# Moving the weight slots and the matmul inputs of a 16-bit-split float32 transformer kernel within SBUF

## The chip, the cores and the metric

The kernel runs on one core of one Trainium2 chip. The metric is the device time of one execution in microseconds (us). A time is the median of several executions; the profile is of one more execution, whose own time is given beside its span.

## The reference, cut to what matters

The input is one sequence of 512 tokens with 1024 features. A first block of four mixers, then two hybrid layers (attention, RWKV-7, retention), each with a feed-forward part. Nearly all arithmetic is in products of the activations with large weight matrices:

```
def first_block(...):
    h = rms_norm(x, norm1_g[l]);  z = h @ w_in[l]
    ...
    x = x + mix @ w_out[l]
    hf = rms_norm(x, norm2_g[l]) @ w_up[l]
    x = x + (jax.nn.gelu(gt) * val) @ w_down[l]
    gate = jax.nn.sigmoid(rms_norm(x, norm3_g[l]) @ w_pg[l])
    x = x + (p[l] @ w_pe[l]) * gate

def hybrid_layer(...):                     # twice
    h = _rms(x) * norm1_g;  proj = h @ w_in
    o_a = sliding_window_attention(...) @ w_attn_o
    o_b = rwkv7_time_mix(...) @ w_rwkv_o
    o_c = retention(...) @ w_ret_o
    x = x + mixed @ w_out
    x = x + (jax.nn.silu(h2 @ w_ffn_gate) * (h2 @ w_ffn_up)) @ w_ffn_down
```

## The kernel before, in words

**The three products.** A float32 product is made of three products in the type fp32r: each operand is split into a high part (the value cast to fp32r) and a low part (what is left). `slot(s, I, a, chunks)` in the TensorE program computes 128 output rows over all 512 tokens: first high weights with high activations, then high weights with low activations, then low weights with high activations, one pass each of 8 chunks (6 in a third of the MLP's down projection, 4 for the outputs of the mixers, 2 for the per-layer embedding). Each matmul has a stationary operand of 128 columns (the weights, out of `w_hi` or `w_lo`) and a moving operand of 512 columns (the activations). All passes go through the helper `mm` at line 547.

**The slots of weights.** `raw`, `w_hi` and `w_lo` have two slots each (`s` is 0 or 1) of 8 x 128 float32 in each partition. SyncE loads a slot of `raw` by one DMA; GpSimd copies it to `w_hi[:, s, 0:n]` (`high_part`, line 370) and subtracts to `w_lo[:, s, 0:n]` (`low_part`, line 377). TensorE runs slot 0, slot 1, slot 0 and so on.

**The moving operands.** `xg_hi`, `xg_lo` hold the normed and scaled input of a layer (8 chunks of 512). `hid_hi`, `hid_lo` hold the MLP's activations (they lie over `z_rt`). `y_hi`, `y_lo` hold the first block's mixer outputs; `y1_hi`, `y1_lo` (over `z_rw`) and `y2_hi`, `y2_lo` (over `z_rt`) those of the hybrid layers. `emb_hi`, `emb_lo` are the embedding's. The trace calls all of the `y` pairs `y_hi`, `y_lo`.

**Where a tensor lies.** Nothing in the kernel allocates by itself: `place(name, shape, dt, offset, line)` hands out byte addresses in a partition one behind the other, rounded up to 32 bytes. With `line=v` it first moves on until the address is `v` modulo `LINE` = 512. A chunk of 512 float32 is 2048 bytes and a block of 128 weights 512 bytes, so all chunks and all blocks of a tensor share one remainder modulo 512.

The order of the work on each engine is written out by hand and depends on no address.

Of the kernel before, what the change touches and what calls it, by code (L numbers as in the profile page):

```python
# [14 lines left out]
F32, F32R, U32 = mybir.dt.float32, mybir.dt.float32r, mybir.dt.uint32  # L15
# [3 lines left out]
P = 128  # L19
T = 512  # L20
NT = T // P
D = 1024
DC = D // P
# [6 lines left out]
LN_EPS = 64e-5  # L30
DECAY = float(np.exp(-0.5))
LINE = 512
WEIGHTS, OTHERS = 128, 160


B1_IN, X_OUT, O_PAIRS, PE_PAIRS = 9, 4, 24, 8
# [71 lines left out]
def build(nc, dram, out):  # L108
    ctx = ExitStack()
    with ctx:  # L110
# [3 lines left out]
        def place(name, shape, dt=F32, offset=None, line=None):  # L114
            n = 4 * int(np.prod(shape))
            if offset is None:
                if line is not None:
                    at[0] += (line - at[0]) % LINE
                offset = at[0]
                at[0] += (n + 31) // 32 * 32  # L120
            return nc.alloc_sbuf_tensor_at(name, [P, *shape], dt, offset=offset), offset

        x, _ = place("x", (DC, T))
        xg_hi, _ = place("xg_hi", (DC, T), F32R)
        xg_lo, _ = place("xg_lo", (DC, T), F32R)
        junk, _ = place("junk", (1,))
        raw, _ = place("raw", (2, DC * P))
        w_hi, _ = place("w_hi", (2, DC * P), F32R, line=WEIGHTS)
        w_lo, _ = place("w_lo", (2, DC * P), F32R, line=WEIGHTS)
        rstd, _ = place("rstd", (T,), line=OTHERS)  # L130
        sumsq, sumsq_at = place("sumsq", (T,))
        K = {}
        for name, shape in KEEP:
# [4 lines left out]
        for name, shape in FIRST:  # L138
            K[name], _ = place(name, shape, U32 if name == "hgmask" else F32)
        z, _ = place("z", (18, T))  # L140
        y_hi, _ = place("y_hi", (DC, T), F32R)
        y_lo, _ = place("y_lo", (DC, T), F32R)
        m1 = {}
        for name, shape in (("ta", (2, T)), ("tb", (2, T)), ("tc", (2, T)), ("td", (2, T + 16)), ("te", (2, T)), ("tf", (2, T)),
                            ("tg", (2, T)), ("th", (2, T))):
# [7 lines left out]
        att, _ = place("att", (2, 2, 4, P))  # L153
        sml, _ = place("sml", (64,))
# [8 lines left out]
        for name, shape in RETAT:  # L163
            K[name], _ = place(name, shape)
        at[0] = max(end, at[0])
        z_rw, rw_at = place("z_rw", (14, T))
        z_rt, rt_at = place("z_rt", (16, T))
        scratch = at[0]
        C4 = 4 * 4 * T

        y1_hi, _ = place("y1_hi", (4, T), F32R, offset=rw_at)
        y1_lo, _ = place("y1_lo", (4, T), F32R, offset=rw_at + C4)
        z_at, _ = place("z_at", (6, T), offset=rw_at + 2 * C4)
        y2_hi, _ = place("y2_hi", (4, T), F32R, offset=rt_at)
        y2_lo, _ = place("y2_lo", (4, T), F32R, offset=rt_at + C4)
        hid_hi, _ = place("hid_hi", (DC, T), F32R, offset=rt_at)
        hid_lo, _ = place("hid_lo", (DC, T), F32R, offset=rt_at + 2 * C4)
        emb_at = base + 24 * 1024
        emb_hi, _ = place("emb_hi", (2, T), F32R, offset=emb_at)
        emb_lo, _ = place("emb_lo", (2, T), F32R, offset=emb_at + C4 // 2)  # L180
        emb, _ = place("emb", (2, T), F32, offset=emb_at + C4)
# [15 lines left out]
        mixed, _ = place("mixed", (DC, T))  # L197
# [3 lines left out]
        turned, _ = place("rt_turned", (8, P), offset=h_at - 4 * T)  # L201
# [2540 lines left out]
```

How the kernel before makes its waits and increments, by code:

```python
        @block.sync  # L301
# [3 lines left out]
                def one(i):  # L305
                    for s in range(2):
                        src = dram[names[s]] if index is None else dram[names[s]][index]
                        n = src.shape[-1]
                        sp.wait_ge(w_split[s], I0 + i + 1)
                        sp.sem_inc(pe_turn, 1)
                        sp.dma_start(raw[:, s, 0:n], src[i + from_pair, s] if len(src.shape) == 4 else src[i + from_pair]).then_inc(raw_in[s], 16)
                with sp.Fori(0, pairs) as i:
                    one(i)
            I = 0
            for c in range(DC):
                sp.dma_start(x[:, c, :], dram["x"][c]).then_inc(x_in[c], 16)
                if c in (0, 3):
                    s = c // 3
                    sp.wait_ge(w_split[s], 1)
                    sp.sem_inc(pe_turn, 1)
                    sp.dma_start(raw[:, s, :], dram["w1_in"][0, s]).then_inc(raw_in[s], 16)
            for name in keep_names:
# [16 lines left out]
                for name, _ in RWKV:  # L340
                    sp.dma_start(K[name][:], dram[name][l] if len(dram[name].shape) > 1 + len(dict(RWKV)[name]) else dram[name]).then_inc(layer_in, 16)
                load(RW_PAIRS - 1, ("w2_rw", "w2_rw"), I + 1, l, 1); I = I + RW_PAIRS
                for n, name in ((RET_PAIRS, "w2_ret"), (AT_PAIRS, "w2_at")):
                    load(n, (name, name), I, l); I = I + n
                sp.wait_ge(s2["done"], l * NT + NT)
                sp.sem_inc(pe_turn, 1)
                for name, _ in RETAT:
```

## Time and profile before

| what | value |
|---|---|
| median of 3 runs | 2564.78 us (2562.37 to 2566.61) |
| the profiled execution's own time | 2564.04 us |
| its span | 2562.2 us |
| TensorE matmuls (PE) busy | 2528.5 us, 99% of the span, 16344 instructions |
| TensorE weight loads (PEld) busy | 2012.7 us, 79% |
| VectorE (DVE), ScalarE (ACT), GpSimd (POOL) busy | 1311.9, 691.3, 1510.1 us |
| mean granted TensorE clock | 0.998 |
| matmuls of the slots (with `w_hi` or `w_lo`) | 9456 |

A matmul's busy time in the profile is longer than the step from one matmul's start to the next one's, since matmuls are pipelined: 512 columns show 389 to 398 ns each, while the starts are some 230 ns apart. The pace is therefore read from the starts in the timeline, never from the mean duration.

### The profile page before, as it was taken

How to read it: one execution, taken by the hardware profiler on the slowest of the kernel's cores; microseconds unless marked ns; L12 is line 12 of the kernel's file. 1: busy time of each engine (PE TensorE's matmuls, PEld its weight loads, DVE VectorE, ACT ScalarE, POOL GpSimd, SP SyncE). 2: the span in 40 equal slices, each digit the busy share in tenths (PEclk: the TensorE clock that was granted, in tenths of full speed). 3: DMA queues.
4: the chain of work that ended last, by engine and by line, in shares of the span. 5: the costliest groups of instructions: out<-in, count | busy, mean ns of one | idle time of the engine just before them, and what ended most of it. 6: DMA issues, size and time to landing. Idle time of an engine off the chain costs nothing.

```text
span 2562.2 us, 47105 instructions
## 1 busy us (share of the span) xinstructions
PE 2528.5 (99%) x16344; PEld 2012.7 (79%) x16344; DVE 1311.9 (51%) x1979; ACT 691.3 (27%) x1290; POOL 1510.1 (59%) x963
## 2 busy tenths in 40 slices
PE   8989999999999999999999999999999999999999
PEld 6868888887877778888888888877778888888887
DVE  7866555455566657763322224566547663322224
ACT  4452000034134446522100002135446521100002
POOL 5666666655646455556666666646455556666665
PEclk9999999999999999999999999999999999999999
DMA  4213222223211132223222223211132223222222
GB/s 166 71 46 115 94 95 98 92 84 116 98 44 52 43 100 73 72 79 103 99 93 96 98 92 120 91 51 52 43 98 71 69 85 103 92 97 98 91 97 99
DMA packets 72442, 222.55 MB, mean 87 GB/s; under 512 B 9312, under 2 KB 12256, under 8 KB 72288
## 3 DMA queue, kind: packets, MB, share of 16 engines
q1 hardware_dynamic: 71856, 220.36, 26.0%
q8 instruction: 96, 1.57, 0.3%
q14 instruction: 58, 0.48, 0.1%
q10 hardware_dynamic: 432, 0.14, 0.0%
HBM read 218.37 MB, written 2.10 MB: 86 GB/s over the span
## 4 chain that ended last, share of the span: by engine, by line
PE 93%; DVE 3%; DVEq 1%; DMA 1%; issue 1%; POOL 1%; ACT 0%; ACTq 0%; POOLq 0%; SPq 0%
PE acc L547 81%; PE bank L547 10%; DMA raw<-in_w_pg 1%; PE bank L1213 0%; POOL w_lo L377 0%; DVE y_lo L1251 0%; DVE sumsq L1251 0%; POOL w_hi L370 0%; DMA vec<-in_vec 0%; DVE xg_lo L1344 0%; DVE att L1463 0%; DVEq L1411 0%; DVEq L1708 0%; DVEq L1464 0%; DVE rw_kp L1732 0%
## 5 line engine op out<-in xcount | busy, mean ns | idle before, releaser
L377 POOL TENSOR_TENSOR w_lo<-raw,w_hi 128x1024 fp32r<-128x1024 f32 (+3 forms) x438 | 962.8, 2198 | 308.5 <-PE acc L547 246.0
L370 POOL TENSOR_SCALAR w_hi<-raw 128x1024 fp32r<-128x1024 f32 (+3 forms) x438 | 434.9, 993 | 596.1 <-PE acc L547 511.5
L547 PE MATMUL acc<-xg_hi,w_hi 128*128 128x512 f32 x2208 | 582.7, 398 | 6.1 <-DVE xg_lo L1344 3.2
L547 PE MATMUL acc<-xg_lo,w_hi 128*128 128x512 f32 x2208 | 569.0, 393 | 0.0
L547 PE MATMUL acc<-xg_hi,w_lo 128*128 128x512 f32 x2208 | 562.6, 393 | 0.2 <-POOL w_lo L377 0.2
L547 PEld LDWEIGHTS acc<-xg_hi,w_hi 128*128 128x128 f32 x2208 | 408.6, 188 | 107.6 <-issue 20.1
L547 PEld LDWEIGHTS acc<-xg_hi,w_lo 128*128 128x128 f32 x2208 | 411.4, 188 | 88.3 <-issue 1.5
L547 PEld LDWEIGHTS acc<-xg_lo,w_hi 128*128 128x128 f32 x2208 | 411.4, 188 | 87.5 <-issue 1.5
L2130 ACT ACTIVATE ffn_act<-ffn_t 128x512 f32<-128x512 f32 x100 | 63.3, 633 | 748.4 <-DVEq L1311 605.7
L1251 DVE TENSOR_TENSOR x<-x,acc 128x512 f32<-128x512 f32 x104 | 71.5, 688 | 323.5 <-PE acc L547 322.9
L1251 DVE TENSOR_TENSOR bank<-acc,rstd 128x512 f32<-128x512 f32 x72 | 50.4, 699 | 263.4 <-PE acc L547 263.2
L547 PE MATMUL acc<-hid_hi,w_hi 128*128 128x512 f32 x656 | 182.4, 396 | 0.1
L547 PE MATMUL acc<-hid_lo,w_hi 128*128 128x512 f32 x656 | 181.6, 395 | 0.0
L547 PE MATMUL acc<-hid_hi,w_lo 128*128 128x512 f32 x656 | 174.7, 395 | 0.0
L1251 DVE TENSOR_TENSOR ffn_t<-acc,rstd 128x512 f32<-128x512 f32 x100 | 69.2, 692 | 196.9 <-PE acc L547 182.2
L547 PEld LDWEIGHTS acc<-hid_hi,w_hi 128*128 128x128 f32 x656 | 123.2, 188 | 31.7 <-DVE hid_lo L1251 1.1
L547 PEld LDWEIGHTS acc<-hid_hi,w_lo 128*128 128x128 f32 x656 | 123.2, 188 | 29.8
L547 PEld LDWEIGHTS acc<-hid_lo,w_hi 128*128 128x128 f32 x656 | 123.2, 188 | 29.4
L2147 ACT ACT_TABLE_LOAD x95 | 121.9, 1283 | 8.9 <-DMA bs<-in_bs 4.6
L2130 ACT ACTIVATE ffn_act<-bank 128x512 f32<-128x512 f32 x22 | 13.2, 599 | 308.2 <-DVEq L1611 308.2
L547 PE MATMUL acc<-y_hi,w_hi 128*128 128x512 f32 x256 | 74.2, 410 | 6.9 <-DVEq L1561 4.8
L2130 ACT ACTIVATE bank<-x,gains 128x512 f32<-128x512 f32 x56 | 38.6, 690 | 148.6 <-DVEq L1284 99.0
(351 smaller groups left out, 2710.8 us busy)
## 6 DMA issues: line engine op xcount, KB each, us to landing
raw<-in_w_up SPq DMA_DIRECT2D x132, 512.0 KB, 3.2
raw<-in_w_down SPq DMA_DIRECT2D x48, 512.0 KB, 3.2
raw<-in_w_gate SPq DMA_DIRECT2D x48, 512.0 KB, 3.2
raw<-in_w_ret SPq DMA_DIRECT2D x32, 512.0 KB, 3.2
raw<-in_w_rw SPq DMA_DIRECT2D x28, 512.0 KB, 3.2
raw<-in_w_o SPq DMA_DIRECT2D x48, 256.0 KB, 2.7
raw<-in_w_in SPq DMA_DIRECT2D x18, 512.0 KB, 3.3
raw<-in_w_down SPq DMA_DIRECT2D x24, 384.0 KB, 3.0
```

The costliest lines, as they stand in the source:

```text
L370: nc.gpsimd.tensor_scalar(w_hi[:, s, 0:n], raw[:, s, 0:n], 1.0, 0.0, ALU.mult, ALU.add).then_inc(w_half[s], 1)
L377: nc.gpsimd.tensor_tensor(w_lo[:, s, 0:n], raw[:, s, 0:n], bits(w_hi[:, s, 0:n]), ALU.subtract).then_inc(w_split[s], 1)
L547: return nc.tensor.matmul(o, a, b, start=first, stop=last, skip_group_check=shared)
L1251: return v.tensor_tensor(o, a, b, op)
L2130: return nc.scalar.activation(o, i, f, **kw)
L2147: nc.scalar.preload_act_table_set(name)
```

## The change

It moves tensors within SBUF and gives the slots of `w_hi` and `w_lo` longer rows. No instruction is added, removed or moved on any engine (TensorE's 1807 listed program rows, VectorE's 982, ScalarE's 648, GpSimd's 295 and SyncE's 224 are the same ones before and after). Only addresses differ.

```diff
-WEIGHTS, OTHERS = 128, 160
+PLACE, PLACE_LO, PLACE_B1 = 128, 192, 384
...
-        xg_hi, _ = place("xg_hi", (DC, T), F32R)
-        xg_lo, _ = place("xg_lo", (DC, T), F32R)
+        xg_hi, _ = place("xg_hi", (DC, T), F32R, line=PLACE)
+        xg_lo, _ = place("xg_lo", (DC, T), F32R, line=PLACE)
...
-        w_hi, _ = place("w_hi", (2, DC * P), F32R, line=WEIGHTS)
-        w_lo, _ = place("w_lo", (2, DC * P), F32R, line=WEIGHTS)
-        rstd, _ = place("rstd", (T,), line=OTHERS)
+        w_hi, _ = place("w_hi", (2, DC * P + 4), F32R, line=PLACE)
+        w_lo, _ = place("w_lo", (2, DC * P + 2), F32R, line=PLACE_LO)
+        rstd, _ = place("rstd", (T,))
...
-        y_hi, _ = place("y_hi", (DC, T), F32R)
-        y_lo, _ = place("y_lo", (DC, T), F32R)
+        y_hi, _ = place("y_hi", (DC, T), F32R, line=PLACE)
+        y_lo, _ = place("y_lo", (DC, T), F32R, line=PLACE)
...
-        z_rw, rw_at = place("z_rw", (14, T))
-        z_rt, rt_at = place("z_rt", (16, T))
+        z_rw, rw_at = place("z_rw", (14, T), line=PLACE_B1)
+        z_rt, rt_at = place("z_rt", (16, T), line=PLACE_LO)
```

Counted through `place`, the addresses modulo 512 are these (bytes within a partition):

| tensor | role | before | after |
|---|---|---|---|
| `xg_hi`, `xg_lo` | moving | 128 | 128 |
| `hid_hi`, `hid_lo`, `y2_hi`, `y2_lo` | moving | 256 | 192 |
| `y1_hi`, `y1_lo` | moving | 256 | 384 |
| `y_hi`, `y_lo` (first block) | moving | 480 | 128 |
| `emb_hi`, `emb_lo` | moving | 192 | 256 |
| `w_hi` slot 0, slot 1 | stationary | 128, 128 | 128, 144 |
| `w_lo` slot 0, slot 1 | stationary | 128, 128 | 192, 200 |
| `rstd`, `sumsq`, `ones`, `headones`, `ident` | others | 160 | 224 |

Every tensor that lies behind `w_hi` is shifted by a few dozen bytes with them. The last address stays inside the partition in both.

## Rows read from the trace of the kernel before

**Rows 1.** The page: busy time per engine, then the span in 40 slices.

```profile
span 2562.2 us, 47105 instructions
PE 2528.5 (99%) x16344; PEld 2012.7 (79%) x16344; DVE 1311.9 (51%) x1979; ACT 691.3 (27%) x1290; POOL 1510.1 (59%) x963
PEclk9999999999999999999999999999999999999999
```

**Rows 2.** The chain of waits that ended last, whole span; then its longest piece.

```profile
PE acc L547 81%; PE bank L547 10%; DMA raw<-in_w_pg 1%; PE bank L1213 0%; POOL w_lo L377 0%; DVE y_lo L1251 0%; DVE sumsq L1251 0%; POOL w_hi L370 0%; DMA vec<-in_vec 0%; DVE xg_lo L1344 0%; DVE att L1463 0%; DVEq L1411 0%; DVEq L1708 0%; DVEq L1464 0%; DVE rw_kp L1732 0%
...
1236.61 327.04 PE acc L547 x1431
```

**Rows 3.** Costliest groups: name, count | busy us, mean ns | idle before, releaser.

```profile
L377 POOL TENSOR_TENSOR w_lo<-raw,w_hi 128x1024 fp32r<-128x1024 f32 (+3 forms) x438 | 962.8, 2198 | 308.5 <-PE acc L547 246.0
L370 POOL TENSOR_SCALAR w_hi<-raw 128x1024 fp32r<-128x1024 f32 (+3 forms) x438 | 434.9, 993 | 596.1 <-PE acc L547 511.5
L547 PE MATMUL acc<-xg_hi,w_hi 128*128 128x512 f32 x2208 | 582.7, 398 | 6.1 <-DVE xg_lo L1344 3.2
L547 PEld LDWEIGHTS acc<-xg_hi,w_hi 128*128 128x128 f32 x2208 | 408.6, 188 | 107.6 <-issue 20.1
L547 PE MATMUL acc<-hid_hi,w_hi 128*128 128x512 f32 x656 | 182.4, 396 | 0.1
L547 PEld LDWEIGHTS acc<-hid_hi,w_lo 128*128 128x128 f32 x656 | 123.2, 188 | 29.8
L547 PE MATMUL acc<-y_hi,w_hi 128*128 128x512 f32 x256 | 74.2, 410 | 6.9 <-DVEq L1561 4.8
```

**Rows 4.** Timeline of TensorE, `xg` slots: start us, busy us, what (28 passes).

```profile
2470.34 1.98 PE L547 MATMUL acc<-xg_lo,w_hi 128*128 128x512 f32 x8
2472.15 1.98 PE L547 MATMUL acc<-xg_hi,w_lo 128*128 128x512 f32 x8
...
2521.11 1.98 PE L547 MATMUL acc<-xg_hi,w_lo 128*128 128x512 f32 x8
```

**Rows 5.** Timeline of TensorE, `hid` slots of 6 chunks, end of the kernel.

```profile
2547.00 1.56 PE L547 MATMUL acc<-hid_hi,w_lo 128*128 128x512 f32 x6
...
2555.40 1.56 PE L547 MATMUL acc<-hid_hi,w_lo 128*128 128x512 f32 x6
```

**Rows 6.** Timeline of TensorE, `y` slots of the first block, then of a hybrid layer.

```profile
157.55 1.10 PE L547 MATMUL acc<-y_lo,w_hi 128*128 128x512 f32 x4
...
161.29 1.09 PE L547 MATMUL acc<-y_hi,w_lo 128*128 128x512 f32 x4
...
1124.80 1.09 PE L547 MATMUL acc<-y_hi,w_hi 128*128 128x512 f32 x4
...
1127.59 1.99 PE L547 MATMUL acc<-xg_hi,w_hi 128*128 128x512 f32 x8
```

**Rows 7.** Timeline of TensorE, an `xg` slot right behind `y` slots.

```profile
1011.58 2.02 PE L547 MATMUL acc<-xg_hi,w_hi 128*128 128x512 f32 x8
1013.44 1.98 PE L547 MATMUL acc<-xg_lo,w_hi 128*128 128x512 f32 x8
1015.25 1.97 PE L547 MATMUL acc<-xg_hi,w_lo 128*128 128x512 f32 x8
```

**Rows 8.** Timeline of the weight loads, three narrow windows in one `hid` pass.

```profile
2554.23 0.19 PEld L547 LDWEIGHTS acc<-hid_lo,w_hi 128*128 128x128 f32 x1
2554.47 0.19 PEld L547 LDWEIGHTS acc<-hid_lo,w_hi 128*128 128x128 f32 x1
2554.70 0.19 PEld L547 LDWEIGHTS acc<-hid_lo,w_hi 128*128 128x128 f32 x1
```

**Rows 9.** Busy time by stretch (span, PE, PEld, DVE, ACT, POOL, clock, DMA).

```profile
205.00:640.00 435.00, 433.04 (x1869) 349.15 (x1867) 250.14 (x345) 64.65 (x101) 270.17 (x171) 1.00 0.29 97
640.00:950.00 310.00, 305.19 (x3652) 229.30 (x3651) 180.28 (x311) 113.47 (x244) 171.65 (x106) 1.00 0.20 67
1119.00:1600.00 481.00, 480.95 (x2099) 392.78 (x2095) 150.81 (x221) 55.14 (x85) 300.82 (x185) 1.00 0.30 99
```

## The prediction, made before the changed kernel ran

> **What bounds the kernel now.** I read the page first. TensorE is busy for 2528.5 of 2562.2 us and its granted clock is at the upper of its two levels, 2.4 GHz, throughout [rows 1]. The chain of waits says the same from the other side: 81% of it are matmuls into `acc`, that is, matmuls of the slots, and one piece of it is 1431 such matmuls in 327.04 us without anything between them, 228.5 ns each [rows 2]. The groups show that TensorE hardly waits: 6.1 us before the first passes with `xg`, 0.1 us before those with `hid`, 6.9 us before those with `y`, while GpSimd, which makes the weights ready, waits for TensorE (511.5 us before the high parts, 246.0 before the low parts) [rows 3]. So the time is the number of matmuls times their pace, and whatever changes the pace of the slots' matmuls changes the time in full.
>
> The pace has to be read from starts. In `xg` slots 28 passes of 8 matmuls take from 2470.34 to 2521.11 us: 50.77 us / 224 = 226.7 ns [rows 4]. In `hid` slots six passes of 6 take from 2547.00 to 2555.40: 8.40 / 36 = 233.3 ns [rows 5]. In `y` slots four passes of 4 take from 157.55 to 161.29: 3.74 / 16 = 233.8 ns, and in a hybrid layer three take from 1124.80 to 1127.59: 2.79 / 12 = 232.5 ns [rows 6]. The 512 columns, at one per cycle of 2.4 GHz, would take 213.3 ns (an estimate from the shape in the rows and the granted clock). So there are 13.4 ns above that in an `xg` matmul and 20.0 in a `hid` matmul. These are instructions of one shape, one type and one clock, with the same 188 ns weight load beside each [rows 3]. What differs between them in the code is the tensor that is streamed, hence its address: `xg` is at 128 modulo 512 like the weights, `hid` and the hybrid `y` at 256, the first block's `y` at 480.
>
> Two more rows say what kind of thing this is. Within a `hid` pass the weight loads start at 2554.23, 2554.47 and 2554.70, steps of about 240 and 230 ns [rows 8]: a long and a short step take turns. And an `xg` slot behind `y` slots needs 1.86 us for its first pass (1011.58 to 1013.44, 232.5 ns each) and 1.81 for its second (226.3 ns) [rows 7]. So the stream has a memory: it takes about one pass to settle into its steady pace, and the steady pace depends on what is streamed. I read this as two readers of SBUF, the moving operand and the load of the next 128 weights, which get in each other's way more or less according to how their addresses stand to each other. The trace can't prove it, as no two rows differ in the address alone.
>
> **The change, part by part.** There are 9456 such matmuls: 3 x 2208 = 6624 with `xg`, 3 x 656 = 1968 with `hid`, 3 x 256 = 768 with `y` [rows 3], and 96 with the embedding and others, which I leave out.
>
> *`hid`.* The distance from the weights to the moving operand goes from +128 bytes (256 - 128) to +64 and +48 over `w_hi` (slots 0 and 1) and to 0 and -8 over `w_lo`. The one distance whose pace is known to be lower is 0, at 226.7 ns. Bounds: the floor of 213.3 ns, -20.0 x 1968 = -39.4 us; above, no row has a steady pace over 233.8, so 0 or +1 us. I take the `xg` pace, the nearest row in distance: -6.6 x 1968 = -13.0 us.
>
> *`y`.* The first block's pairs come to 128 and thus have all four distances of `xg`; `y2` goes with `hid`; `y1` goes to 384, +256 and +240 over `w_hi` and +192 and +184 over `w_lo`, of which no row speaks. Bounds -20.0 x 768 = -15.4 and 0. I take 6.6 ns for all: -5.1 us.
>
> *`xg`.* Slot 0's two passes with `w_hi` keep distance 0. Slot 0's pass with `w_lo` gets -64, slot 1's get -16, -16 and -72. So 4 of the 6 passes of a pair of slots change: 6624 x 4/6 = 4416 matmuls. This is the large term, and no row shows it. Bounds: the floor, -13.4 x 4416 = -59.2 us; and the pace of `hid`, +6.6 x 4416 = +29.1 us. That these are small distances beside a distance whose pace is the lowest measured speaks for a value near 0; that 13.4 ns are left above the floor even there, and that the most which an address has been seen to give is 6.6, makes room below. I take -1.5 ns, an average of passes that stay and of some that gain: -6.6 us.
>
> *The longer rows and the shift of all the rest.* GpSimd writes and reads the same number of elements; its two operations take 0.99 and 2.20 us, 3.2 us for a slot [rows 3], against 3 x 1.81 = 5.4 us that TensorE works on one, so even a tenth more on them stays under TensorE. In the stretch of the feed-forward part GpSimd is busy for 300.82 of 481.00 us, VectorE for 150.81 [rows 9]. The cover is gone only where TensorE's slot falls below 3.2 us, and no bound above comes near. The DMAs write `raw`, whose address stays. The smaller matmuls (attention, RWKV, retention) stream from tensors that shift too; they are 10% of the chain, and half a percent of that either way is 1.3 us. I put it at 0 and keep it for the range. Nothing is queued behind a new wait, as no wait is added.
>
> The sum: -13.0 - 5.1 - 6.6 = -24.7 us on the profiled execution's own time, 2564.0 us (span 2562.2), which stands 0.7 us under the median of the runs: 2539.3, in round numbers **2540 us**.
>
> A rule of the Trainium skill speaks against all of this. TensorE: Matmul & The Clock Gate, section "Step-by-step: what each phase is for", says that TensorE has two independent SBUF read ports, so that loading the next weights takes nothing from the running matmul. By it placement would be worth nothing and the time would stay at 2564. The trace doesn't bear it out as a reason for equal paces: `xg` and `hid` differ by 6.6 ns. And SBUF — State Buffer, "Specifications (TRN2)", gives lines of 16 bytes and a penalty for each crossing to a new one: `w_lo`'s slot 1, at 8 bytes past such a line, would touch 33 instead of 32 of them for 128 weights. No run here shows what that costs, and the sum doesn't use it.
>
> **The rivals.**
>
> *No change.* The 6.6 ns belong to something else, for example to what VectorE and ScalarE do during those slots, or to the pass lengths of 6 and 4. Against it: VectorE is busier in the stretch from 205 to 640 us (250.14 of 435.00) than from 1119 to 1600 (150.81 of 481.00) [rows 9], and the slots keep their pace to the hundredth of a microsecond over 28 passes [rows 4]. The time is then 2564.
>
> *Slower: the steady state is lost.* Before, every pass with `xg` has one distance, and the stream may stay settled for 28 passes and more [rows 4]. After, the distance changes twice in each slot and again from slot to slot: 0, 0, -64, -16, -16, -72. If each distance has its own steady phase, and settling takes about a pass at 232.5 ns [rows 7], the stream never settles. That puts 5.8 ns on 6624 matmuls, +38.4 us, while `hid` and `y` stay where they are, since they are that slow already: 2602 us. If only the changed passes suffer, 5.8 x 4416 = +25.6, with `hid` gaining its 13.0: 2577 us. It decides from the point where the `xg` pace rises by more than 18.1 / 6624 = 2.7 ns, to over 229.4. For it: the long memory in rows 7 and 8. Against it: distances of 16 and 72 bytes are small beside the 128 and 352 that cost 6.6 ns.
>
> *Much faster: a lower steady pace exists.* The paces seen are 226.7 and 233.3, 6.6 ns apart; one such step further is 220.1, still above the floor of 213.3. If the small negative distances reach it, the 4416 changed `xg` matmuls give 6.6 x 4416 = -29.1 and `hid` and `y` 13.2 x 2736 = -36.1: 2564.0 - 65.2 = 2499 us. At the floor it would be -59.2 - 54.8: 2450 us. For it: the 13.4 ns that nothing else explains. Against it: no row has a steady pace below 226.
>
> **How the numbers follow.** The forecast (2525 to 2556 us: `hid` and `y` gain between half and all of their 18.1, `xg` between 0 and 20) 0.40; much faster (under 2525) 0.20; no change 0.12; slower (2570 to 2602) 0.28. Differences under 0.2%, 5 us, can't be told from none in this kernel. Faster therefore has 0.60, same 0.12, slower 0.28. For 8 in 10, I leave out the half of the much faster case near the floor (below 2490) and the part of the slower one in which nothing at all is won (above 2588): 2490 to 2588. The likeliest case's own range is 2525 to 2556.
>
> **What would show it.** The timeline of `hid` passes of 6 should take 1.36 us instead of 1.40, those of `y` 0.91 instead of 0.93. The passes of `xg` should be 1.81 us or a little less, with a visible difference between slots 0 and 1 or between the passes with `w_hi` and `w_lo`. TensorE's count, its idle time before the passes and GpSimd's 0.99 and 2.20 us should stay. The prediction is wrong if the `xg` passes take over 1.84 us (the lost steady state), if `hid` stays at 233 ns (address not the cause, or the wrong distance), or if the `xg` passes fall under 1.78 us (a lower steady pace).

## The result, and the profile after

The changed kernel takes 2582.46 us (median of 4 runs, 2580.86 to 2583.04) against 2564.41 (4 runs): a ratio of 1.0069, 95% interval 1.0052 to 1.0087. It is slower, by 18 us or 0.7%. The forecast was 2540 us and faster; the range of 2490 to 2588 held the time, but the side was wrong.

The page after, its first rows and the groups that answer to [rows 1, 3]:

```profile
span 2581.2 us, 47105 instructions
PE 2549.7 (99%) x16344; PEld 2018.0 (78%) x16344; DVE 1312.0 (51%) x1979; ACT 691.5 (27%) x1290; POOL 1511.7 (59%) x963
PEclk9999999999999999999999999999999999999999
L377 POOL TENSOR_TENSOR w_lo<-raw,w_hi 128x1024 fp32r<-128x1024 f32 (+3 forms) x438 | 963.7, 2200 | 320.8 <-PE acc L547 259.1
L547 PE MATMUL acc<-xg_hi,w_hi 128*128 128x512 f32 x2208 | 591.2, 402 | 4.2 <-DVE xg_lo L1344 2.7
```

The same instructions, the same clock, GpSimd's subtraction 2200 ns where it was 2198, and no more idle time on TensorE before its passes (4.2 us before the first ones with `xg`, 6.1 before). GpSimd waits longer for TensorE (259.1 us before that operation, 246.0 before). So the 19.0 us by which the span grew are pace. The longest piece of the chain shows them, 1431 matmuls in 331.15 us instead of 327.04 [rows 2], 231.4 ns each instead of 228.5:

```profile
1245.48 331.15 PE acc L547 x1431
```

TensorE's timeline shows in which passes. The columns are start, busy time and what ran. A pass takes the step to the next row's start, and the pace is that step over the row's count:

```profile
2486.61 2.01 PE L547 MATMUL acc<-xg_hi,w_hi 128*128 128x512 f32 x8
2488.46 1.98 PE L547 MATMUL acc<-xg_lo,w_hi 128*128 128x512 f32 x8
2490.27 2.03 PE L547 MATMUL acc<-xg_hi,w_lo 128*128 128x512 f32 x8
2492.14 2.03 PE L547 MATMUL acc<-xg_hi,w_hi 128*128 128x512 f32 x8
2494.01 2.02 PE L547 MATMUL acc<-xg_lo,w_hi 128*128 128x512 f32 x8
2495.87 2.03 PE L547 MATMUL acc<-xg_hi,w_lo 128*128 128x512 f32 x8
2497.74 2.01 PE L547 MATMUL acc<-xg_hi,w_hi 128*128 128x512 f32 x8
...
2563.34 1.55 PE L547 MATMUL acc<-hid_hi,w_hi 128*128 128x512 f32 x6
...
2571.63 1.55 PE L547 MATMUL acc<-hid_hi,w_hi 128*128 128x512 f32 x6
```

Before, each `xg` pass took 1.81 us [rows 4]. Now the two slots differ: slot 0 takes 1.85, 1.81, 1.87 and slot 1, which is the one ahead of `hid` at the end of the stretch, 1.87, 1.86, 1.87: 11.13 us for a pair of slots instead of 10.88. Only one pass in six is as it was, slot 0's second, which lies at distance 0 and comes from distance 0. Five of six are over the 1.84 us that the prediction named as its sign of being wrong. The `hid` passes go the other way, 8.29 us for 36 matmuls, 230.3 ns instead of 233.3 [rows 5].

Added up over the whole trace, from each matmul's start to the next one's, gaps included, by moving tensor (us; matmuls into `acc` alone, and the last `hid` one has no next):

| kernel | `xg` x6624 | `y` x768 | `hid` x1967 | span |
|---|---|---|---|---|
| before | 1567.0 | 186.9 | 459.9 | 2562.2 |
| changed | 1591.8 | 187.8 | 454.3 | 2581.2 |
| difference | +24.8 | +0.9 | -5.6 | +19.0 |

### The profile page after: what moved, and what is told of

Same layout as the page of the kernel before. It is cut to its first block, busy times and chain, and to the rows that moved or that the text cites. A ratio compares the mean times of both kernels' runs of the same rounds, so it can differ in the third digit from the quotient of the medians.

```text
span 2581.2 us, 47105 instructions
## 1 busy us (share of the span) xinstructions
PE 2549.7 (99%) x16344; PEld 2018.0 (78%) x16344; DVE 1312.0 (51%) x1979; ACT 691.5 (27%) x1290; POOL 1511.7 (59%) x963
## 4 chain that ended last, share of the span: by engine, by line
PE 92%; DVE 4%; DVEq 2%; issue 1%; DMA 1%; POOL 1%; ACT 0%; ACTq 0%; POOLq 0%; SPq 0%
PE acc L547 80%; PE bank L547 10%; DMA raw<-in_w_pg 1%; PE bank L1213 0%; DVE z L1251 0%; POOL w_lo L377 0%; DVE y_lo L1251 0%; DVE sumsq L1251 0%; DVE m_ta L1409 0%; DMA vec<-in_vec 0%; DVEq L1445 0%; DVE xg_lo L1344 0%; DVE att L1463 0%; POOL w_hi L370 0%; DVE m_tg L1251 0%
## 5 line engine op out<-in xcount | busy, mean ns | idle before, releaser
L377 POOL TENSOR_TENSOR w_lo<-raw,w_hi 128x1024 fp32r<-128x1024 f32 (+3 forms) x438 | 963.7, 2200 | 320.8 <-PE acc L547 259.1
L547 PE MATMUL acc<-xg_hi,w_hi 128*128 128x512 f32 x2208 | 591.2, 402 | 4.2 <-DVE xg_lo L1344 2.7
L547 PE MATMUL acc<-xg_hi,w_lo 128*128 128x512 f32 x2208 | 576.2, 398 | 0.3 <-POOL w_lo L377 0.3
L2130 ACT ACTIVATE ffn_act<-bank 128x512 f32<-128x512 f32 x22 | 13.2, 599 | 312.4 <-DVEq L1611 312.4
```

The costliest lines, as they stand in the source:

```text
L377: nc.gpsimd.tensor_tensor(w_lo[:, s, 0:n], raw[:, s, 0:n], bits(w_hi[:, s, 0:n]), ALU.subtract).then_inc(w_split[s], 1)
L547: return nc.tensor.matmul(o, a, b, start=first, stop=last, skip_group_check=shared)
L2130: return nc.scalar.activation(o, i, f, **kw)
```

## The experiments

My theory after the result: the distance between the moving operand and the weights, in bytes, sets the pace, and going from one distance to another costs extra. "Distance" is moving minus stationary address, as in the prediction. The rivals: the moving tensor's own address sets it (theory 2 below); address is not the cause (theory 3); or the longer rows are the whole cost. In what follows "settling" is the short stretch after a change of distance in which the pace moves to its new steady value.

**e1_pace_sweep: the disputed pace by itself**

```diff
...
+for n, (m, s) in enumerate(CASES):   # bytes by which the moving and the stationary operand are shifted
+    with pe.Fori(0, 5):
+        for k in range(8):
+            nc.tensor.matmul((even, odd)[n % 2], weights[:, k * P + s // 4:(k + 1) * P + s // 4],
+                             moving[:, k * T + m // 4:(k + 1) * T + m // 4], ...)
```

> This kernel leaves out the whole computation and only streams matmuls of the slots' form (128x128 fp32r stationary, 512 moving columns, 8 blocks and 8 chunks in turn), 40 for each placement: both operands start at 128 modulo 512, then the stationary one is shifted by 0 to 496 bytes in steps of 16 (and by 4, 8, 24, 72), the moving one by 64 to 448 (and 16, 32, 48), and both together by 8 to 352. Theory 1 (the distance between the two sets the pace): both together leaves 226.7 ns; stationary +64 and +16 alone give 233.3; moving +128 alone gives 233.3. Theory 2 (the moving operand's own remainder sets it): shifting the stationary one does nothing (226.7 at all), both together by 128 gives 233.3. Theory 3 (address is not the cause): 226.7 at every placement. A steady pace under 226 at any placement would mean that a better place exists.

This kernel, e5 and e9 ran once each. While their matmuls run, no other engine works.

The order of the cases is forward, then (0, 0), then backward. TensorE's timeline, 40 matmuls a row; "even" and "odd" take turns so that each case has its row:

```profile
21.84 9.23 PE L150 MATMUL even<-moving,weights 128*128 128x512 f32 x40
30.91 9.24 PE L150 MATMUL odd<-moving,weights 128*128 128x512 f32 x40
39.99 9.48 PE L150 MATMUL even<-moving,weights 128*128 128x512 f32 x40
49.31 9.49 PE L150 MATMUL odd<-moving,weights 128*128 128x512 f32 x40
58.64 9.49 PE L150 MATMUL even<-moving,weights 128*128 128x512 f32 x40
...
170.06 9.25 PE L150 MATMUL even<-moving,weights 128*128 128x512 f32 x40
179.15 9.24 PE L150 MATMUL odd<-moving,weights 128*128 128x512 f32 x40
...
355.35 9.32 PE L150 MATMUL even<-moving,weights 128*128 128x512 f32 x40
364.51 9.45 PE L150 MATMUL odd<-moving,weights 128*128 128x512 f32 x40
373.80 9.50 PE L150 MATMUL even<-moving,weights 128*128 128x512 f32 x40
...
475.25 9.23 PE L150 MATMUL odd<-moving,weights 128*128 128x512 f32 x40
484.33 9.28 PE L150 MATMUL even<-moving,weights 128*128 128x512 f32 x40
493.44 9.50 PE L150 MATMUL odd<-moving,weights 128*128 128x512 f32 x40
502.78 9.51 PE L150 MATMUL even<-moving,weights 128*128 128x512 f32 x40
...
993.31 9.48 PE L150 MATMUL odd<-moving,weights 128*128 128x512 f32 x40
1002.63 9.25 PE L150 MATMUL even<-moving,weights 128*128 128x512 f32 x40
```

Read as steps over 40: distance 0 (21.84 to 30.91) 226.8 ns; -16 (30.91) 227.0; -32 (39.99) 233.0; -48 (49.31) 233.3; -256 (170.06) 227.3. With the moving operand shifted, +64 (355.35) 229.0 and +128 (364.51) 232.3. With both shifted together, by 256 (475.25) 227.0 and by 352 (484.33) 227.8, settling included. The same case -16 on the way back, coming from -32 (993.31 to 1002.63): 233.0. Two of the cases shifted together stand out: by 16 bytes (493.44) 233.5, on the way back 230.0, and by 8 (502.78) 233.7, and 233.5 on the way back.

The mean over the last 24 matmuls of a case, where the pace is steady, in ns: 0: 226.7; -4: 232.5; -8: 230.7; -16: 227.0 or 232.9; -24: 229.9; -32, -48, -64, -72: 233.1 to 233.5; -96: 234.1; -128: 232.2 or 233.4; -160: 233.3; -176: 230.0; -192: 229.0; -240: 228.3 or 227.0; -256: 226.7; and the steps from -256 to -496 repeat those from 0 to -240 to 0.2 ns, but for the second state at -240. +64: 228.9, +128: 232.1 or 232.6, +192: 233.3, +256: 226.7, +320: 228.9. +16: 231.7 both ways; +32: 233.3; +48: 233.0 or 233.3. The stationary shifts not named here lie between 231.9 and 233.5; -208, the same distance as +48 modulo 256, has 232.1 or 231.9.

So theory 1 holds as to distance, with three additions that I had not expected. The pace repeats every 256 bytes, not 512. Some placements, -16 first of all, have two states, of which the way in selects one. And distance is not all where the moving operand is an odd multiple of 16 bytes off: +16 has 231.7, while -240, the same distance modulo 256 made by shifting the weights, has 228.3 or 227.0. Theory 2 falls (shifting the stationary operand alone costs 6.6 ns), and theory 3 too. In this sweep the moving operand has to sit on a multiple of 32 bytes for the full pace: shifts of 32, 64, 128, 256 and 352 together are fast, 16 and 8 together are not. The stationary one need not, since -16 has 227.0 when entered from 0. No placement has a steady pace under 226.7, so my rival "much faster" had nothing to win: before, `xg` already had the best place there is in this sweep.

**e2_all_at_128: the slow tensors of the kernel before at distance 0**

```diff
+        y_hi, _ = place("y_hi", (DC, T), F32R, line=128)
+        y_lo, _ = place("y_lo", (DC, T), F32R, line=128)
...
+        z_rw, rw_at = place("z_rw", (14, T), line=128)
+        z_rt, rt_at = place("z_rt", (16, T), line=128)
```

> The kernel before with the moving tensors of the down projections and of the mixers' outputs (z_rw, z_rt, y_hi, y_lo) also at 128 modulo 512, where the weights and xg are; nothing else. Theory 1 (distance 0 is the fast one): hid and y passes fall from 233.3 to 226.7 ns, 2736 x 6.6 = -18 us: 2546 us. Theory 3 (address not the cause): 2564.

2548.92 us, ratio 0.9950 (0.9933 to 0.9966). Six passes of 6 in `hid`:

```profile
2530.03 1.52 PE L547 MATMUL acc<-hid_hi,w_lo 128*128 128x512 f32 x6
...
2538.19 1.52 PE L547 MATMUL acc<-hid_hi,w_lo 128*128 128x512 f32 x6
```

8.16 / 36 = 226.7 ns, as forecast. In the count from start to start `hid` falls from 459.9 to 447.9 us and `y` from 186.9 to 184.1; `y` gains 2.8 of the 5.1: in its steps of under 300 ns the mean falls from 232.8 to 227.6 ns, less than 6.6, and the longer steps, 20.5 us before and 22.5 here, don't gain. The time is 3 us over the 2546 expected.

**e3_low_only and e4_pads_only: the two halves of the weights' move, alone**

```diff
-        w_lo, _ = place("w_lo", (2, DC * P), F32R, line=WEIGHTS)
+        w_lo, _ = place("w_lo", (2, DC * P), F32R, line=192)      # e3
...
-        w_hi, _ = place("w_hi", (2, DC * P), F32R, line=WEIGHTS)
-        w_lo, _ = place("w_lo", (2, DC * P), F32R, line=WEIGHTS)
+        w_hi, _ = place("w_hi", (2, DC * P + 4), F32R, line=WEIGHTS)      # e4
+        w_lo, _ = place("w_lo", (2, DC * P + 2), F32R, line=WEIGHTS)      # e4
```

> The kernel before with only w_lo moved by 64 bytes (192 modulo 512), all other remainders as before, no longer rows. Theory 1: the 2208 xg matmuls with w_lo go from 226.7 to 233.3 ns (+14.6 us), and the 2208 with w_hi and xg_hi that follow lose some 4 ns each in settling (+9 us): 2586 to 2588. Rival (the longer rows are what costs in the change): 2564.

2576.02 us, ratio 1.0047 (1.0030 to 1.0064): +11.3 us, half of what I expected. `xg` counts 1583.1 us, +16.1 where I had 24: in steps under 300 ns its passes with `w_lo` go from 227.3 to 233.2 ns, nearly as forecast, but those with `w_hi` and `xg_hi` behind them only from 228.0 to 229.9, not by 4. `hid`, whose low passes come to +64, gains 2.6, which I had left out. Those low passes show the memory again: in the slots from 1200 us on they take turns at 228.8 and 233.0 ns, though both slots have the same distances.

> The kernel before with only the longer rows, 4 and 2 elements, so slot 1 lies 16 bytes (w_hi) and 8 bytes (w_lo) off; all tensors at their old remainders. Theory 1: slot 1's passes lose some 4 to 6 ns on half of the xg matmuls, +13 to +20 us: 2577 to 2584, and slot 0 pays for settling on top. Rival (distances under 64 bytes don't matter, w_lo's 64 is the cost): 2564 to 2567.

2571.23 us, ratio 1.0026 (1.0015 to 1.0036): +6.5 us, also under the forecast. `xg` counts 1573.9, +6.9. The expectation failed for `w_hi`'s row: in the slots from 2466 us on, slot 1's two passes at -16 stay at 226.7 and 226.9 ns. Only `w_lo` at -8 (230.8 ns) and the pass behind it, which settles (231.2), lose. Each half costs something; neither is the whole.

**e5_weight_columns and e9_moving_columns: what the loss goes with**

e5 loads 128, 64 or 32 stationary columns under 512 moving ones; e9 streams 512, 448, 384 or 256 columns under 128 or 32.

The edit against e1's helper, as e9 has it (`n` stationary and `w` moving columns; in e5 `w` is 512):

```diff
-nc.tensor.matmul(o[:], weights[:, k * P + s // 4:(k + 1) * P + s // 4], moving[:, k * T + m // 4:(k + 1) * T + m // 4], ...)
+nc.tensor.matmul(o[0:n, 0:w], weights[:, k * P + s // 4:k * P + n + s // 4], moving[:, k * T + m // 4:k * T + w + m // 4], ...)
```

> The sweep's kernel again, which leaves out the whole computation, now with 128, 64 or 32 stationary columns under the same 512 moving ones, at distances 0, -64, +128 and -192. If the load of the next weights is what holds the moving operand up, the time above 213.3 ns goes with the columns loaded: at distance 0 13.4 ns with 128, some 7 with 64 and 3 to 4 with 32; at the slow distances 20, 10 and 5, so that distance matters little at 32 columns. If the loss belongs to the moving operand alone, the pace of each distance stays what it is with 128 columns.

Timeline of e5, distance 0, then the start of the next case:

```profile
28.91 9.23 PE L150 MATMUL odd<-moving,weights 128*128 128x512 f32 x40
37.98 9.36 PE L150 MATMUL even<-moving,weights 128*64 128x512 f32 x40
47.17 9.43 PE L150 MATMUL odd<-moving,weights 128*32 128x512 f32 x40
56.44 9.49 PE L150 MATMUL even<-moving,weights 128*128 128x512 f32 x40
```

226.8, 229.8 and 231.8 ns for 128, 64 and 32 columns. At distance 0 loading less makes it slower; at -64 it makes it a little faster (233.3, 232.8, 231.6). Both of my expectations fail: the time above 213.3 ns does not go with the columns loaded, and the pace does not stay either. At 32 columns all four distances lie between 230.7 and 231.8, so how much a distance is worth does depend on the load's length. My picture of two readers who collide, for a time that grows with what is read, is not right as it stands.

> The sweep's kernel, which leaves out the whole computation, with 512, 448, 384 or 256 moving columns, 128 or 32 stationary ones, at distances 0 and -64. If the loss is a fixed piece for each matmul, the pace at distance 0 is columns/2.4 plus 13.3 ns: 226.7, 200, 173.3, 120. If it goes with the moving columns streamed, it is columns x 226.7/512: 226.7, 198.3, 170, 113.3. With 256 columns the weight load of 128 may become the bound.

Timeline of e9: distance 0 (28.96 to 57.88), then distance -64 (from 86.87):

```profile
28.96 9.23 PE L150 MATMUL odd<-moving,weights 128*128 128x512 f32 x40
38.02 8.27 PE L150 MATMUL even<-moving,weights 128*128 128x448 f32 x40
46.13 7.12 PE L150 MATMUL odd<-moving,weights 128*128 128x384 f32 x40
53.09 4.95 PE L150 MATMUL even<-moving,weights 128*128 128x256 f32 x40
57.88 9.42 PE L150 MATMUL odd<-moving,weights 128*32 128x512 f32 x40
...
86.87 9.49 PE L150 MATMUL odd<-moving,weights 128*128 128x512 f32 x40
96.20 8.25 PE L150 MATMUL even<-moving,weights 128*128 128x448 f32 x40
104.29 7.09 PE L150 MATMUL odd<-moving,weights 128*128 128x384 f32 x40
111.22 4.70 PE L150 MATMUL even<-moving,weights 128*128 128x256 f32 x40
115.76 9.40 PE L150 MATMUL odd<-moving,weights 128*32 128x512 f32 x40
```

At distance 0 with 512, 448, 384 and 256 columns: 226.5, 202.8, 174.0, 119.8 ns; at -64: 233.3, 202.3, 173.3, 113.5. Above columns / 2.4 that is some 13, 16, 13 and 13 ns, and 20, 16, 13 and 7. At distance 0 the loss is about a fixed piece for each matmul, as the first expectation had it; at -64 it shrinks with the columns, and neither expectation fits. Which distance is the good one depends on the number of columns: at 256 the distance that costs 512-column matmuls 6.6 ns is the better one by 6, on the way back too (120.0 and 113.6 ns). The way in matters here as well: 448 columns at distance 0 have 202.8 ns at first and 206.5 on the way back, behind 384 columns.

**e6_inputs_only and e7_at_384: the moving tensors alone**

```diff
+        y_hi, y_lo: line=128;  z_rw: line=384;  z_rt: line=192      # e6, weights as before
+        y_hi, y_lo, z_rw, z_rt: line=384                            # e7, weights as before
```

> The kernel before with only the moving tensors where the change puts them (y_hi, y_lo at 128, z_rw at 384, z_rt at 192), weights as before. By the sweep (229.0 ns at distance +64, 226.7 at 0 and at +256): hid -4.3 ns x 1968 = -8.5 us, y -6.6 ns x 576 and -4.3 ns x 192 = -4.6 us: 2551 to 2552. If only the absolute place of the moving tensor counts, y1 at 384 and hid at 192 have no reason to gain: 2563 to 2564.

2553.73 us, ratio 0.9957 (0.9941 to 0.9974), 2 us over the forecast. `hid` counts 452.0 us, and the mean of its steps under 300 ns is 229.0, which is the sweep's pace at +64; `y` counts 183.6. This third of the change is good by itself.

> As e2_all_at_128, but z_rw, z_rt, y_hi and y_lo at 384 modulo 512, 256 bytes from the weights. If the pace repeats every 256 bytes of distance, as the sweep shows, this is as fast as e2: 2549 us. If 512 were the period, hid and y would have a pace of their own, 233 ns, and the time would be 2564.

2546.87 us, ratio 0.9929 (0.9912 to 0.9945), against e2's 2548.92. The two intervals overlap; 256 bytes off is as good as 0, in this kernel too.

**e8_after_no_pads: the changed kernel without the longer rows**

```diff
-        w_hi, _ = place("w_hi", (2, DC * P + 4), F32R, line=PLACE)
-        w_lo, _ = place("w_lo", (2, DC * P + 2), F32R, line=PLACE_LO)
+        w_hi, _ = place("w_hi", (2, DC * P), F32R, line=PLACE)
+        w_lo, _ = place("w_lo", (2, DC * P), F32R, line=PLACE_LO)
```

> The changed kernel without the longer rows: w_lo at 192, hid at 192, y1 at 384, y at 128. By the sweep hid has +64, +64, 0 (229.0, 229.0, 226.7) in place of e3's +128, +128, +64, some -3.7 ns x 1968 = -7 us, and y some -3 us: 2566 from e3's 2576. The longer rows thus cost some 16 us in the changed kernel (2582.5), more than the 6.5 they cost in the kernel before. If the parts simply add, this is 2564.7 + 11.3 plus what e6 shows.

2570.91 us, ratio 1.0023 (1.0013 to 1.0032), 5 us over the 2566 expected: against e3 `hid` falls by 5.4 us (I had 7) and `y` by 1.5 (I had 3). So the longer rows cost 11.6 us in the changed kernel, not 16, and 6.5 in the kernel before. The parts do not add: e3, e4 and e6 alone are +11.3, +6.5 and -11.2, some 7 us together, and the whole change is 18. Two slots of its timeline:

```profile
2478.61 2.03 PE L547 MATMUL acc<-xg_hi,w_lo 128*128 128x512 f32 x8
2480.47 2.00 PE L547 MATMUL acc<-xg_hi,w_hi 128*128 128x512 f32 x8
2482.32 1.98 PE L547 MATMUL acc<-xg_lo,w_hi 128*128 128x512 f32 x8
2484.13 2.03 PE L547 MATMUL acc<-xg_hi,w_lo 128*128 128x512 f32 x8
2485.99 2.00 PE L547 MATMUL acc<-xg_hi,w_hi 128*128 128x512 f32 x8
```

The pass with `w_lo` at -64 takes 1.86 us. The pass after it is back at distance 0 and takes 1.85 all the same: that is settling (its eight steps are 231, 230, 236, 229, 232, 231, 227 and 226 ns). Only the one after that has 1.81. So a shifted `w_lo` costs two passes of three.

**e10_w_hi_row, e11_w_lo_row, e12_after_w_hi_row: each row apart, and where the stream comes from**

```diff
+        w_hi, _ = place("w_hi", (2, DC * P + 4), F32R, line=WEIGHTS)   # e10, on e2; w_lo at line=384, OTHERS 416
+        w_lo, _ = place("w_lo", (2, DC * P + 2), F32R, line=WEIGHTS)   # e11, on e2
+        w_lo, _ = place("w_lo", (2, DC * P), F32R, line=PLACE_LO)      # e12, on the changed kernel
```

> e2_all_at_128 with only w_hi's rows 4 elements longer, so slot 1's high halves are at distance -16 (w_lo at 384 modulo 512, distance -256, which is as good as 0). The sweep had two states at -16: 227.0 ns when it came from distance 0, 232.9 when it came from -32. If what came before decides, slot 1 stays at 227 and the time is e2's 2549; if not, slot 1's passes with w_hi lose 6.3 ns on a third of 9360 matmuls, 2568.

> e2_all_at_128 with only w_lo's rows 2 elements longer, so slot 1's low halves are at distance -8. The sweep has 230.6 ns there, from both sides: 4 ns on a sixth of 9360 matmuls, +6 us, and the pass that follows has to settle again, up to 5 ns on another sixth, +8: 2555 to 2563. If only distances of 16 bytes and more mattered, 2549.

> The changed kernel with w_lo's rows back at their length, so that of the longer rows only w_hi's is left (slot 1's high halves at distance -16 from xg, its low halves at -64 as slot 0's). In e10 the same row cost nothing, as the stream came into slot 1 from distance 0. Here it comes from w_lo at -64. If what came before decides (the sweep: 232.9 ns at -16 when coming from another distance), slot 1's passes with w_hi lose up to 6.3 ns on 2208 xg matmuls: 2577 to 2583, as slow as the changed kernel. If w_hi's row costs nothing anywhere and w_lo's 8 bytes are the whole cost of the rows, the time is e8's: 2571.

e10: 2548.16 us, 0.9933 (0.9916 to 0.9950). e11: 2557.05, 0.9970 (0.9958 to 0.9983). e12: 2582.29, 1.0070 (1.0056 to 1.0084). The same 4 elements in `w_hi`'s rows cost nothing where slot 1 is entered from distance 0 (e10 against e2, with `xg` at 1566.0 and 1565.9 us), and 11.4 us where it is entered from -64 (e12 against e8), while `w_lo`'s 2 elements cost 8.1 us on e2 and nothing more in the changed kernel (2582.46 against 2582.29). One slot of e10 and the start of the next, then slot 1 of e12 and the start of the next:

```profile
2480.61 1.98 PE L547 MATMUL acc<-xg_hi,w_hi 128*128 128x512 f32 x8
2482.42 1.98 PE L547 MATMUL acc<-xg_lo,w_hi 128*128 128x512 f32 x8
2484.23 1.98 PE L547 MATMUL acc<-xg_hi,w_lo 128*128 128x512 f32 x8
2486.05 1.98 PE L547 MATMUL acc<-xg_hi,w_hi 128*128 128x512 f32 x8
```

```profile
2479.32 2.03 PE L547 MATMUL acc<-xg_hi,w_hi 128*128 128x512 f32 x8
2481.19 2.03 PE L547 MATMUL acc<-xg_lo,w_hi 128*128 128x512 f32 x8
2483.06 2.03 PE L547 MATMUL acc<-xg_hi,w_lo 128*128 128x512 f32 x8
2484.92 2.00 PE L547 MATMUL acc<-xg_hi,w_hi 128*128 128x512 f32 x8
```

In e10 every pass takes 1.81 us, whichever slot it is. In e12 slot 1's two passes with `w_hi` take 1.87 each. Not all of e12's 11.4 us are this: `xg` rises by 7.4 (1583.0 to 1590.4), `hid` by 3.4 (451.9 to 455.3), for whose slot 1 the row changes +64 (228.9 ns in the sweep) into +48 (232.1 in the sweep where it is the weights that are 16 bytes off, at -208). I had not set this second part out in the expectation, and had the first at up to 14.

## Why the prediction was wrong

**What bounds the kernel, and that pace is the whole effect:** right. Counts, clock, idle time and GpSimd stayed; the 19 us are 20.1 us of pace in the three families of passes, less 1.1 in the rest.

**That the pace depends on the distance:** right, and now shown, as long as the moving operand sits on a multiple of 32 bytes. e1 moves one operand or both and nothing else, and has the 6.6 ns with no other engine at work; e2's passes of 6 run at 226.7 ns. So neither the other engines nor the length of a pass, the causes named in the rival "no change", are needed. The memory read from [rows 7, 8] is real as well: e1's -16 has 227.0 or 233.0 ns by the way in, and e8's pass behind `w_lo` settles for 1.85 us.

**The step that failed is the term for `xg`,** "-1.5 ns, an average of passes that stay and of some that gain: -6.6 us". It is +24.8 us: 3.7 ns on each of 6624 matmuls, or 5.6 on each of the 4416 that change. Two things in it were wrong. I wrote that small distances beside the best one measured speak for a value near 0; -64 has the full slow pace of 233.3, and -32 too. And I took the 13.4 ns left above 213.3 as room that a better place could use, though no row had a pace under 226; the sweep has none either, and in e9 some 13 ns are left at 384 columns at either distance. Four of six passes went off the best point, and a fifth, slot 0's first with `w_hi`, pays for settling: 1.85 us at distance 0. By the sweep alone the pair of slots would be 226.7, 226.7, 233.3, 232.9, 232.9, 233.3: a mean of 231.0; the timeline has 11.13 us / 48 = 231.9, and the whole trace 231.6 outside long gaps.

**The term for `hid`:** the sign right, the size too large: -5.6 us for -13.0. I gave all of it the pace of distance 0. The sweep has 228.9 at +64, 232.1 at +48 (made as here, with the weights 16 bytes off), 226.7 at 0 and 230.7 at -8: weighted by passes (2, 2, 1, 1 of 6) 229.9. The rows show 230.3; passes of 6 at distance 0 behind +64 take 229.7 ns, so settling covers the rest.

**The term for `y`:** -5.1 forecast, +0.9 measured. With the weights left alone it is -3.3 (e6), with `w_lo` moved too -1.0 (e8) and with the longer rows as well +0.9, so the weights' move took it away.

**The rival that came true** is "slower: the steady state is lost", to which I gave 0.28, at 2577 to 2602 us. Its mechanism is about half of the story. Over the twelve slots from 2475 us on, slot 0's passes are at 231.0, 226.5 and 233.9 ns and slot 1's at 233.6, 232.8 and 233.3, which is 31.5 ns over six times 226.6. Of these, 4.4 are settling in slot 0's first pass. Another 13.2 are slot 1's passes at -16, which are slow only because they are entered from -64: entered from 0 they have 226.7 and 226.9 in e4. The other 14.0 are the passes with `w_lo`, since -64 and -72 have slow steady paces of their own whatever came before, which I had held to be unlikely. That part of the loss is missing from the rival, and it had `hid` gain 13.0 or nothing, not 5.6; that its 2577 to 2602 held 2582 is partly luck. The crossing point named with it, an `xg` pace over 229.4 ns, was passed.

**The Trainium skill's rule** that loading weights takes nothing from the running matmul (TensorE: Matmul & The Clock Gate, "Step-by-step: what each phase is for") does not mean here that placement is free: e1 has 226.7 and 233.3 ns for the same two instructions. Nor does loading only 32 columns take away the time above 213.3 ns (e5), so the simplest opposite, a collision in proportion to the load, is refuted too. Lines of 16 bytes (the Trainium skill, SBUF — State Buffer, "Specifications (TRN2)") could explain at most that 8 bytes are bad (230.7 ns at -8), and no run isolates even that; they don't explain that both operands shifted by 16 are slow and both by 32 fast.

What stays open is the mechanism below this: why distance modulo 256, why a grid of 32 bytes for the moving operand, what the two states are, and why the good distance changes with the number of columns.

The experiments give a kernel that beats both: `w_hi`, `w_lo`, `xg`, `hid` and all `y` at one remainder modulo 256, 2546.87 us (e7) or 2548.92 (e2), 1.4% under the changed kernel.

## What to carry to other kernels

Where TensorE is the bound and streams fp32r with 128 stationary and 512 moving columns, put the stationary and all moving tensors at one remainder modulo 256 bytes, a multiple of 32, and keep a slot's row a multiple of 256 too: it is worth up to 3% of a matmul and costs some padding. For other column counts it has to be measured anew; at 256 moving columns the order was the other way round. Measure such a pace from starts in the timeline, in a sweep kernel of some 1 ms, before changing the layout: the best point may already be in use, and a gap to the peak is not by itself something that the layout can win. Judge parts of a layout in their context, since the same 16 bytes cost `xg`'s passes nothing or 7.4 us here, by what the stream came from.

## What the hardware showed that I had not expected

- Several steady paces, the fastest and many of the slow ones, are whole multiples of 6.67 ns: 34 of them at distance 0 and 35 at -64 with 512 columns (226.7, 233.3), 26 with 384 (173.3), 18 or 17 with 256 (120.0 at distance 0, 113.3 at -64). Where long and short steps take turns, as in [rows 8], two of them make 70: 0.47 us. Others are not, such as 228.9 at +64 and 230.7 at -8.
- The pace has a memory over matmuls: e1's -16 stays at 227.0 for 40 matmuls when it comes from 0 and at 232.9 when it comes from -32. Both operands shifted by 16 have 233.4 coming from 352 and 229.9 coming from 8.
- Fewer stationary columns under 512 moving ones are slower at distance 0: 226.8, 229.8, 231.8 ns for 128, 64, 32.
